# The first rows of w_ada in two passes around x, and three projection groups that begin with feature pair 0 alone

## The reference

```python
c_act = jax.nn.silu(c)                       # c: (1, 2048)
mod = c_act @ w_ada[l] + b_ada[l]            # w_ada: (2048, 6 * 2048)
sh1, sc1, gt1, sh2, sc2, gt2 = jnp.split(mod, 6, axis=-1)
h = modulate(rms_norm(x, g_mix[l]), sh1, sc1)    # h * (1 + scale) + shift
z = h @ w_in[l]                              # w_in: (2048, 11344)
```

## Time and profile before

| | us |
|---|---|
| median of 3 runs | 2667.49 |
| lowest to highest | 2667.02 to 2667.75 |
| profiled execution | 2666.06 |
| its span | 2664.2 |

### The profile page before, as it was taken

One profiled execution on the slowest core, in us unless ns is written; L12 is line 12 of the kernel. 1 busy time (PEld: TensorE's weight loads), 2 busy tenths in 40 slices (PEclk: granted clock), 3 DMA queues, 4 the chain that ended last, 5 costly groups with the idle time before them and its releaser, 6 DMA issues.

```text
span 2664.2 us, 33329 instructions
## 1 busy us (share of the span) xinstructions
PE 2625.6 (99%) x12045; PEld 2164.4 (81%) x12045; DVE 1798.2 (67%) x2072; ACT 1297.8 (49%) x1574; POOL 230.2 (9%) x164
## 2 busy tenths in 40 slices
PE   5999999999999999999999999999999999999999
PEld 3888887888888888888888887887888888888887
DVE  7978777878776677776766855677555555555554
ACT  4455544455454444444444554556454444444443
POOL 0000000100000000000001210240001111111110
PEclk9999999999999999999999999999999999999999
DMA  9989768678867766666665666644666666666663
GB/s 382 401 308 340 243 209 281 196 237 283 304 211 241 220 220 219 218 218 216 218 195 177 198 178 181 190 143 132 199 186 193 190 189 189 190 190 191 191 191 134
DMA packets 280792, 585.61 MB, mean 220 GB/s; under 512 B 22033, under 2 KB 24493, under 8 KB 279797
## 3 DMA queue, kind: packets, MB, share of 16 engines
q1 hardware_dynamic: 280340, 583.61, 68.1%
q10 hardware_dynamic: 352, 0.71, 0.1%
HBM read 582.07 MB, written 2.11 MB: 219 GB/s over the span
## 4 chain that ended last, share of the span: by engine, by line
PE 96%; DVE 2%; DMA 1%; ACT 0%; issue 0%; DVEq 0%; ACTq 0%
PE lin L499 30%; PE lin L501 30%; PE lin L500 30%; DMA sb_ada<-in_w_ada_dram 1%; PE aux L812 1%; PE aux L499 1%; PE aux L501 1%; PE aux L500 1%; PE aux L533 1%; PE aux L986 0%; PE aux L823 0%; DVE sb_wlo L1617 0%; DVE sb_acc L1708 0%; PE aux L557 0%; PE aux L999 0%
## 5 line engine op out<-in xcount | busy, mean ns | idle before, releaser
L1617 DVE TENSOR_TENSOR sb_wlo<-sb_raw,sb_whi 128x1024 fp32r<-128x1024 f32 x896 | 1114.8, 1247 | 784.8 <-ACT sb_whi L1041 781.2
L1041 ACT ACTIVATE sb_whi<-sb_raw 128x1024 fp32r<-128x1024 f32 x896 | 948.9, 1060 | 1237.2 <-PE lin L501 1159.1
L499 PE MATMUL lin<-sb_whi,sb_act_hi 128*128 128x512 f32 x2620 | 1038.4, 396 | 1.9 <-DVE sb_wlo L1617 1.0
L501 PE MATMUL lin<-sb_whi,sb_act_lo 128*128 128x512 f32 x2620 | 1021.8, 390 | 0.0
L500 PE MATMUL lin<-sb_wlo,sb_act_hi 128*128 128x512 f32 x2620 | 1020.7, 390 | 0.0
L499 PEld LDWEIGHTS lin<-sb_whi,sb_act_hi 128*128 128x128 f32 x2620 | 492.5, 188 | 108.5 <-issue 9.3
L501 PEld LDWEIGHTS lin<-sb_whi,sb_act_lo 128*128 128x128 f32 x2620 | 492.1, 188 | 104.3
L500 PEld LDWEIGHTS lin<-sb_wlo,sb_act_hi 128*128 128x128 f32 x2620 | 492.7, 188 | 99.9 <-issue 1.9
L499 PE MATMUL lin<-sb_whi,sb_hid_hi 128*128 128x512 f32 x704 | 275.3, 391 | 0.0
L501 PE MATMUL lin<-sb_whi,sb_hid_lo 128*128 128x512 f32 x704 | 274.1, 389 | 0.0
L500 PE MATMUL lin<-sb_wlo,sb_hid_hi 128*128 128x512 f32 x704 | 274.0, 389 | 0.0
(11 more groups left out here) (362 smaller groups left out, 1819.5 us busy)
## 6 DMA issues: line engine op xcount, KB each, us to landing
sb_raw<-in_w_in_dram SPq DMA_DIRECT2D x176, 512.0 KB, 6.7
sb_raw<-in_ffn_w_gu_dram SPq DMA_DIRECT2D x176, 512.0 KB, 3.7
sb_ada_in<-in_w_ada_dram SPq DMA_DIRECT2D x128, 512.0 KB, 5.1
sb_raw<-in_gla_w_in_dram SPq DMA_DIRECT2D x96, 512.0 KB, 3.8
sb_raw<-in_w_gate_dram SPq DMA_DIRECT2D x88, 512.0 KB, 3.8
sb_raw<-in_w_up_dram SPq DMA_DIRECT2D x88, 512.0 KB, 4.4
sb_raw<-in_w_down_dram SPq DMA_DIRECT2D x88, 512.0 KB, 4.4
sb_raw<-in_ffn_w_down_dram SPq DMA_DIRECT2D x88, 512.0 KB, 3.6
```

The costliest lines, as they stand in the source:

```text
L499: pe.matmul(o, h, whi[:, w], start=first and q == 0, stop=False)
L501: m = pe.matmul(o, l, whi[:, w], start=False, stop=last and q == 1)
L1041: act.activation(whi[:, idx % RING * HALF:(idx % RING + 1) * HALF], raw[:, idx // 2 % RING, idx % 2 * HALF:(idx % 2 + 1) * HALF], ACT.Copy ...
L1617: dve.tensor_tensor(wlo[:, c], raw[:, idx // 2 % RING, idx % 2 * HALF:(idx % 2 + 1) * HALF], whi[:, c].bitcast(fp32), ALU.subtract).then_i ...
```

## The change

The first pass over w_ada is cut in two. The first takes blocks 0 and 1 alone (pair 0; 256 KB a row block, two runs of 1 KB a row), around x as before. The second takes blocks 2 to 5 (512 KB, two runs of 2 KB a row): twelve pieces ahead of half 0, one behind half 0, one behind half 1, two behind half 2 (`SECOND_AT`). TensorE sums pair 0's columns right behind the transposes. Groups 0, 1 and 2 take pair 0 alone, one half each, keep their banks open, and then take pairs 1 and 2; behind half 1 and half 2 stand the columns of blocks 2, 3 and 4, 5. VectorE adds the last four second pieces between the first splits and makes pair 1 behind split 3. The columns of the late blocks, the pairs 3 to 7 and the index projection move on by one half. With the constants given, `A_SUMMED` is empty and `A_DRAINS` is 11, the number of first drains before.

```diff
-CHUNKS = ((0, 2), (2, EARLY), (EARLY, KT))
-EARLY_ROWS = KT + 1
+CHUNKS = ((0, 2), (2, 4), (4, EARLY), (EARLY, KT))
+EARLY_ROWS = 2 * KT + 1
+A_SOLO = 3
+A_DRAINS = GROUPS + A_SOLO - 2 * A_HELD
+A_SUMMED = range(A_SOLO, 2 * A_SOLO - A_HELD)
...
+    plan = [(g, 0, n, True, n < A_SOLO - A_HELD) for n, g in enumerate(A_GROUPS[:A_SOLO])]
+    for n in range(A_SOLO - A_HELD, A_SOLO):
+        plan += [(A_GROUPS[n], p, n, False, p == A_PAIRS - 1) for p in range(1, A_PAIRS)]
...
+LATE_FROM = 4
+SECOND_AT = (12, 13, 14, 16)
+LATE_SUMMED = 39
+LATE_PAIRS = 42
...
-    ada0 = at("ada0", [P, SLOTS, 2 * EARLY * P], ARENA)
+    ada0 = at("ada0", [P, SLOTS, 2 * 2 * P], ARENA + 24 * KB)
+    ada2 = at("ada2", [P, SLOTS, 2 * (EARLY - 2) * P], ARENA)
...
+        def second_piece(kt):
+            sp.wait_ge(sem("ada0_sum"), KT - SLOTS + kt + 1)
+            sp.dma_start(ada2[:, kt % SLOTS, :].rearrange("p (b n) -> p b n", b=2), w_first[kt * P:(kt + 1) * P, :, 2 * P:EARLY * P]
...
+        for kt in range(SECOND_AT[0]):
+            second_piece(kt)
         for i in range(A_ENDS[-1]):
             first_half(i)
+            if i < A_SOLO:
+                for kt in range(SECOND_AT[i], SECOND_AT[i + 1]):
+                    second_piece(kt)
...
+        pe.wait_ge(sem("ada0_sum"), KT)
+        first_columns(0)
...
+            if i in (A_SOLO - 2, A_SOLO - 1):
+                c = i - A_SOLO + 3
+                pe.wait_ge(sem("ada0_sum"), 2 * KT - 1 + c)
+                first_columns(c)
...
+        for kt in range(KT):
             early_add(kt)
+            if kt == 8:
+                norm_stats(0)
+        for kt in range(SECOND_AT[0]):
+            second_add(kt)
+            if kt == 4:
+                first_modulation(0)
+                dve.wait_ge(sem("gs_made"), 1)
+                first_affine(0)
             if kt == 6:
+                first_low(0, xaff[:, 0, :, :])
...
+        for i in range(A_SOLO):
+            for kt in range(SECOND_AT[i], SECOND_AT[i + 1]):
+                hk.setdefault(i, []).append(last_adds if kt == KT - 1 else lambda kt=kt: second_add(kt))
+        hk.setdefault(A_SOLO, []).append(second_pair)
+        hk.setdefault(A_SOLO + 1, []).append(lambda: first_low(2, xT[:, 4:6, :]))
```

More of the change, by code:

```diff
@@ L569, in _ @@
         pe.wait_ge(sem("tt_free"), KT // 2)
[L570 to L575, removed]
         def first_columns(n):
             k0, k1 = CHUNKS[n]
-            acc, c0, w, wide = (acc1, 0, KT - EARLY, WIDE // 4) if n == 2 else (acc0, k0 * P, k1 - k0, WIDE // 2)
+            acc, c0, w, wide = (acc1, 0, KT - EARLY, WIDE // 4) if n == 3 else (acc0, k0 * P, k1 - k0, WIDE // 2)
             for j in range(2 * w):
@@ L589, in keep_running @@
                 pe.matmul(lin[0][0][:], ident, con[:, 0:NB], start=True, stop=True)
-        pe.wait_ge(sem("ada0_sum"), KT - 3)
-        keep_running(3)
[L593 to L598, removed]
+        pe.wait_ge(sem("ada0_sum"), KT)
+        first_columns(0)
+        pe.wait_ge(sem("par_in"), 8 * 16)
+        for n, rws in ((1, 120), (2, 116)):
+            m = pe.transpose(aux[2][:, n % 2 * P:n % 2 * P + rws], parr[0:rws, n, :], ident[0:rws, 0:rws])
+        m.then_inc(sem("par_T"), 1)
+        pe.wait_ge(sem("rel_in"), 32)
+        pe.matmul(aux[3][0:NH, :], relb[:], onehot[:], start=True, stop=True).then_inc(sem("par_T"), 1)
+        pe.wait_ge(sem("ada0_sum"), KT + SECOND_AT[0] - 3)
+        keep_running(3)
         pe.wait_ge(sem("par_cols"), 2)
@@ L654, in _ @@
         first_banks = (lin[1], lin[0], aux[2:4])
[L655 to L666, removed]
+        made = 0
+        for i, (g, p, a, first, last) in enumerate(A_HALVES):
+            n = a - A_DRAINS
+            banks = lin[n % 2] if n >= A_HELD else first_banks[a % 3]
+            if first and a >= 3:
+                pe.wait_ge(free0, A_DRAINS + 1 + n if n >= A_HELD else a)
+                pe.wait_ge(free1, A_DRAINS + 1 + n if n >= A_HELD else a)
+            if p == made:
+                made += 1
+                pe.wait_ge(sem("tt_lo"), made)
+            half(0, "A", A_ENDS[-1], i, 0, 2 * p, first, last, banks=banks)
+            if i in (A_SOLO - 2, A_SOLO - 1):
+                c = i - A_SOLO + 3
+                pe.wait_ge(sem("ada0_sum"), 2 * KT - 1 + c)
+                first_columns(c)
             if i == LATE_SUMMED:
                 pe.wait_ge(sem("ada0_sum"), EARLY_ROWS + 2 * KT)
-                first_columns(2)
-            if i == A_ENDS[0] - 1:
+                first_columns(3)
+            if i == A_ENDS[0]:
                 project_ix()
-            if i == A_ENDS[0] + 2:
+            if i == A_ENDS[0] + 3:
                 wix_turn()
@@ L1173, in late_pair @@
         def late_pair(g):
-            act.wait_ge(sem("gs_made"), 3)
+            act.wait_ge(sem("gs_made"), 4)
             first_pair(g)
-        hk = {A_PAIRS * (n + 1) + 3: [lambda n=n: first_drain(n)] for n in range(GROUPS - A_HELD)}
+        hk = {A_SOLO + g - 1: [lambda g=g: first_features(g)] for g in range(1, A_PAIRS)}
+        for a in range(A_DRAINS):
+            if a not in A_SUMMED:
+                hk.setdefault(A_LAST[a] + (1 if a < A_SOLO - A_HELD else 3), []).append(lambda a=a: first_drain(a))
         for n in range(A_HELD):
@@ L1207, in _ @@
                     hk.setdefault(at + off, []).append(lambda h=h, step=step: step(h))
-        body(0, "A", A_ENDS[-1], hk, start=RING)
+        body(0, "A", A_ENDS[-1], hk, start=0)
         def hold_q(p):
```

136 lines of the change are left out of this document (78 added, 58 removed).

## The result

The changed kernel takes 2673.18 us (median of 18 runs, 2672.09 to 2674.44), the kernel before on the same chip 2667.77 us (2666.14 to 2669.22). The ratio is 1.0021, with a 95% interval of 1.0014 to 1.0027: +5.4 us, slower at the edge of what a measurement of this kernel can tell. The forecast was 2672.6. The profiled execution took 2674.09 us.

What follows compares the result with a forecast made beforehand. The transfer queue was taken to set the pace up to half 36. A +2.5 and B +2.6, with C and D nothing, gave +5.1 us on the median 2667.49, so 2672.6 us; range 2667.3 to 2676.3.

Steps and rivals of the forecast that it cites:

- The rule: Transfer queue ahead of half 36: every microsecond it is empty or slower moves half 36 and the end by that microsecond.
- A: First pieces shrink to 256 KB, so the queue runs empty while SyncE issues the ten small loads: net +2.5 us.
- B: Pieces of w_ada in shorter runs, 4096 more at 10 ns each over 16 engines: +2.6 us.
- C: More vector adds (34.7 us for 30.2) delay TensorE's first halves; covered by transfer delay, costs nothing, 2.1 us if uncovered.
- D: Late columns, late pairs and index projection moved one half later: nothing, bounds -0.5 to +1 us.
- Runs cost nothing: Rival on the transfers: shorter runs cost nothing by themselves, only the hole counts; +3.3 us, 2670.8 us, chance 0.18.
- The hole does not open: Rival on the queue at the small loads: backlog outlasts them and the lead holds; -1.5 us, 2666.0 us, chance 0.10.
- TensorE or VectorE takes over: Rival at half 36: clock drops behind TensorE's stops and VectorE's delay exceed the cover; +8.0 us, 2675.5 us, chance 0.08.

Runs made afterwards that it cites:

- e4: Changed kernel with the 32 late pieces spread behind halves 4 to 38 instead of 4 to 35; 2671.47 us, ratio 1.0015 to the kernel before.
- e7: Changed kernel with ten slots of 256 KB instead of six and the small loads behind the last first piece; 2671.00 us, ratio 1.0014.
- e1: Changed kernel with the ten small loads issued behind the sixth second piece instead of the tenth first piece; 2672.21 us, ratio 1.0020.
- e10: e8 with second pieces 1 to 14 added on half of their columns only; 2667.62 us, ratio 1.0001 to the kernel before.
- e8: Changed kernel with the edits of e7 and e4 together; 2668.23 us, ratio 1.0000 to the kernel before.
- e6: Kernel before, with pieces 6 to 9 of the first pass waiting for the add before last, so the queue runs dry; 2675.04 us, ratio 1.0028.
- e2: Changed kernel reading each first-pass piece as one run per row instead of two, with wrong columns of w_ada; 2670.95 us, ratio 1.0014.
- e9: e8 with six spare matmuls of 512 columns between half 1 and the sums of blocks 2 and 3; 2670.55 us, ratio 1.0014.
- e3: Changed kernel with the edits of e1 and e2 together; 2672.20 us, ratio 1.0016 to the kernel before.

## Why the prediction was right

*The rule* (a microsecond of empty or slow queue ahead of half 36 is a microsecond of time) held: +6.1 and +5.7 us at half 36, +5.4 us in time, and the table above. The reading beside it that TensorE needs 2.75 us a half was 0.03 too high, as short waits still lie in the stretch it was taken from: in e4, without waits, it is (162.04 - 63.98)/36 = 2.72 us from half 4 to the late columns, so the kernel before's own line on TensorE was about 146.3 at half 36 and not 147.3.

*A* came out at its size, with a cause that was only half seen. Forecast: drained at 16.9, flow again at 20.65, +2.5 us net. Measured: the rate falls between 17 and 18 us and is back at 21; over 17 to 21 us 0.41 MB moved instead of 1.61, 3.0 us, less the 1.2 us that the small loads cost before; and 22 to 26 us at 274 instead of the forecast's 345 GB/s, 0.7 us more. That is 2.5 us, and e7, which takes away the hole and the shallow slots at once, gives 2.6 to 3.1 at half 36. What the step did not say: six slots of 256 KB, refilled at the adds' 0.84 us, are a limit of their own of some 300 GB/s. e1 took the small loads away from there and got next to nothing; with ten slots the same stretch moves at 348 instead of 286 GB/s. Two smaller misses stood against each other: the small loads took 3.9 us of issue, not 4.75, and the chain began 1.05 us later, as TensorE's transpose of the small vectors, which comes ahead of it, waited for their last transfer until 10.42 (9.37 before).

*B* was right in the rate, 348 GB/s for the extrapolated 345, and too high in the sum: long runs bring back 0.9 to 1.4 us of the 2.6, which is about the half that the second pass has of it; the first pass is not limited by the queue. Yet e7 leaves 3.6 us missing beside A, and no run has its slots and long runs together. Some of it is there early: by 15 us 15 x (338 - 315) = 0.35 MB are missing, 0.9 us, and 15 to 17 us run at 286 GB/s, 0.6 us more, together 1.5 where the step had 1.1 for these pieces; that the slots' pace and the later start of the adds cause it is argued, not shown. So the right total owes something to luck: two errors of opposite sign, B too high and a slow first pass that no step had in full.

*C* was right where it decided nothing. First matmul 48.50 and 47.60 for 47, half 3 at 59.82 for 59.0, TensorE's own line at 151.0 (e4) for 149.8, all behind the queue's 153.2 to 153.7. From 59.82 at 2.72 us a half the changed kernel's own line would be near 149.7, an estimate without e4's fall of the clock. In the changed kernel VectorE works without idle time from 30.59 to 58.3 us, as the step has it. But e10 shows that less work for VectorE brings the last sums 0.4 us and no more, as the weights come next; that VectorE alone makes this line is not shown. What is left of it in e8 with A gone, 1.1 us, is less than the 1.5 us that half 2 loses to the clock there.

*D*, nothing at the places moved, was some 0.3 to 0.5 us too low: so much is lost behind half 36 in every kernel with the change. The stretch near half clock behind the late columns, which was to stay as it is, cost 1.6 us more in one of two executions of the changed kernel, but it does so in a variant of the kernel before too (e6). No run shows why.

*Rivals.* Runs cost nothing: fallen (e7, e2). The hole does not open: fallen (68 GB/s). TensorE or VectorE takes over: not in this kernel, where the clock does not fall behind the stop (half 2 takes 59.02 - 56.18 = 2.84 us), but its mechanism is real, since e4 and e8 stand on it, with a clock of 0.57 behind the stop for the sums.

## What to carry to other kernels

Cutting the first pieces smaller to start an engine earlier shrinks the backlog that hides every other issue on that queue: count slots times bytes against the time of what is queued behind, and against the pace at which slots are freed. Bytes that come late ahead of the point where two limits meet are late in the end, however early the first matmul starts. When a fix for one limit brings nothing (e1), look at the rate that is left: here it was the pace at which the adds freed the slots.

## What was not expected of the hardware

- A granted clock near 1.2 GHz followed a stop and eight short matmuls in e8 (a stop of 1.46 us, 0.57 over 54 to 58 us), e1 (1.66) and e4 (1.40), and not in e9 without the stop (1.00 over 56 to 60 us), nor with the shorter stops of four other executions, nor in e3 with the longest, 1.67. In e10 it followed an idle stretch of 1.84 us ahead of the first half (0.57 over 46 to 50 us).
- The stretch of low clock behind 40 short matmuls differs between executions of one kernel, and takes one of two sizes: a granted clock of 0.91 or 0.83 over 160 to 180 us in all fourteen traces, 1.6 us of span apart.
- A matmul of 512 columns on plain fp32 operands is two instructions of 0.44 us at full clock (e9); on rounded operands it is one, and twelve of them take 2.72 us (e4), 0.23 us each.
- The transfers hold 402 GB/s over 79 us on this one core, and 411 with runs of 4 KB (e2). The Trainium skill, DMA: Bandwidth & Descriptors, Specifications, gives about 358 GB/s as the limit of HBM per core, which the page's part on bandwidth reads as the share with both cores of an HBM domain streaming; no run here has a second core streaming, and this one alone moves more than that.
